# One level of Strassen in the last two large products of an fp32 encoder layer

## The reference, cut to what matters

```
h = rms_norm(x, norm_g)
u = h @ attn_w_in                        # (256 x 4096) @ (4096 x 10240): q, k, v, z
o = windowed attention of q, k, v        # 32 heads of 128, 8 groups of keys, a sink per head
x1 = x + (o * silu(z)) @ attn_w_out      # (256 x 4096) @ (4096 x 4096)   the OUT product
gate = sigmoid(rms_norm(x1, ple_g) @ ple_w_gate)   # (256 x 4096) @ (4096 x 4096)   the GATE product
out = x1 + (p @ ple_w_proj) * gate       # (256 x 256) @ (256 x 4096)     the small product
```

## Time and profile before

| | us |
|---|---|
| median of 3 runs (lowest, highest) | 1695.78 (1695.72, 1696.10) |
| the profiled execution: its own time | 1696.34 |
| its span, first to last instruction | 1694.5 |
| PE busy | 1676.8 (99% of the span) |
| DVE busy | 945.7 (56%) |
| ACT busy | 800.2 (47%) |
| DMA, mean rate | 189 GB/s |

### The profile page before, as it was taken

How to read it: one execution, slowest core, us unless ns; L and a number is a source line. 1 busy time by engine, 2 the same in 40 slices (tenths; PEclk the granted TensorE clock), 3 DMA queues, 4 the chain that set the end, 5 groups by cost and what they waited for, 6 DMA issues and landing times.

```text
span 1694.5 us, 21692 instructions
## 1 busy us (share of the span) xinstructions
PE 1676.8 (99%) x7648; PEld 1394.9 (82%) x7648; DVE 945.7 (56%) x1008; ACT 800.2 (47%) x1002; POOL 65.4 (4%) x49
## 2 busy tenths in 40 slices
PE   7999999999999999999999999999999999999997
PEld 6888888888888888888888888888888888888886
DVE  7654466565756566565656754444446544444445
ACT  7443445454444545455455544444446444444442
POOL 1000000000000000000000000000000000000005
PEclk9999999999999999999999999999999999999999
DMA  8666665656565565656555566666666666566665
GB/s 298 195 189 194 194 180 168 188 158 186 162 184 173 169 178 162 196 155 189 166 174 173 179 207 203 199 199 201 205 199 200 191 193 193 192 197 190 195 193 179
DMA packets 168584, 319.67 MB, mean 189 GB/s; under 512 B 10592, under 2 KB 14944, under 8 KB 168544
## 3 DMA queue, kind: packets, MB, share of 16 engines
q1 hardware_dynamic: 165376, 314.61, 60.8%
q10 hardware_dynamic: 3168, 4.51, 0.8%
HBM read 314.89 MB, written 4.19 MB: 188 GB/s over the span
## 4 chain that ended last, share of the span: by engine, by line
PE 97%; POOL 1%; DVE 1%; ACT 1%; DMA 0%; issue 0%; POOLq 0%; SPq 0%; ACTq 0%
PE bank L860 31%; PE bank L862 31%; PE bank L861 31%; POOL stage L292 1%; PE bank L931 1%; PE bank L883 1%; PE bank L875 1%; PE bank L921 0%; PE bank L920 0%; PE bank L919 0%; PE bank L939 0%; PE bank L941 0%; PE bank L940 0%; DVE w_lo L555 0%; DMA raw<-in_w_in_dram 0%; ACT w_hi L304 0%
## 5 line engine op out<-in xcount | busy, mean ns | idle before, releaser
L555 DVE TENSOR_TENSOR w_lo<-raw,w_hi 128x1024 fp32r<-128x1024 f32 x584 | 715.3, 1226 | 674.2 <-ACT w_hi L304 673.0
L304 ACT ACTIVATE w_hi<-raw 128x1024 fp32r<-128x1024 f32 x584 | 619.3, 1061 | 753.2 <-PE bank L862 748.5
L860 PE MATMUL bank<-w_lo,aT_hi 128*128 128x512 f32 x2304 | 901.9, 391 | 8.5 <-DVE w_lo L555 8.5
L862 PE MATMUL bank<-w_hi,aT_lo 128*128 128x512 f32 x2304 | 897.9, 390 | 0.0
L861 PE MATMUL bank<-w_hi,aT_hi 128*128 128x512 f32 x2304 | 897.5, 390 | 0.0
L860 PEld LDWEIGHTS bank<-w_lo,aT_hi 128*128 128x128 f32 x2304 | 433.3, 188 | 96.5 <-issue 8.5
L862 PEld LDWEIGHTS bank<-w_hi,aT_lo 128*128 128x128 f32 x2304 | 433.1, 188 | 90.7
L861 PEld LDWEIGHTS bank<-w_hi,aT_hi 128*128 128x128 f32 x2304 | 433.5, 188 | 88.2
L278 POOL TENSOR_TENSOR rstd<-ssq,mhalf 128x8 f32<-128x8 f32 x8 | 13.5, 1682 | 790.5 <-DVE ssq L606 790.5
L668 DVE SCALAR_TENSOR_TENSOR arena<-bank,rstd,arena 128x256 f32<-128x256 f32 x64 | 26.6, 478 | 25.2 <-PE bank L921 15.7
L355 ACT ACTIVATE arena<-arena,nm 128x256 f32<-128x256 f32 x64 | 31.8, 499 | 11.8 <-DVE sd L681 11.8
(11 more groups left out here) (92 smaller groups left out, 551.9 us busy)
## 6 DMA issues: line engine op xcount, KB each, us to landing
raw<-in_w_in_dram SPq DMA_DIRECT2D x320, 512.0 KB, 3.7
raw<-in_w_out_dram SPq DMA_DIRECT2D x128, 512.0 KB, 3.7
raw<-in_w_gate_dram SPq DMA_DIRECT2D x128, 512.0 KB, 3.6
stage<-in_xT_dram SPq DMA_DIRECT2D x8, 512.0 KB, 8.2
arena<-in_x_dram ACTq DMA_DIRECT2D x8, 512.0 KB, 6.5
raw<-in_w_proj_dram SPq DMA_DIRECT2D x8, 512.0 KB, 3.6
out_dram<-stage SPq DMA_DIRECT2D x16, 256.0 KB, 2.0
arena<-in_pT_dram ACTq DMA_DIRECT2D x1, 256.0 KB, 2.7
```

The costliest lines, as they stand in the source:

```text
L304: nc.scalar.activation(w_hi[:, i % RING, :], raw[:, i % RING, :], ACT.Copy).then_inc(hi_done, 1)
L555: nc.vector.tensor_tensor(w_lo[:, i % RING, :], raw[:, i % RING, :], w_hi[:, i % RING, :].bitcast(F32), ALU.subtract).then_inc(lo_done, 1)
L860: nc.tensor.matmul(outs[t][:, :], ahi, wlo, start=first and jj == 0, stop=False)
L862: last = nc.tensor.matmul(outs[t][:, :], alo, whi, start=False, stop=final and jj == 1)
```

## The change

Output columns are now taken 1024 at a time (a pair, four in each stage; `PAIRS`), and weights 256 rows by 1024 columns at a time (a quad; 16 to a pair). A dense quad is two units of 12 matmuls. A Strassen quad takes the 2 x 2 blocks of activations (two blocks of channels by two token tiles) and the 2 x 2 blocks of weights, and makes 7 products of sums of blocks in place of 8, in four units of 1, 2, 2 and 2 products. Quads with odd number from 9 on in the first pair of a stage, and from 3 on in the other three pairs, are Strassen quads: 4 + 3 x 7 = 25 in a stage, 50 in all. So dense and Strassen quads alternate.

Each Strassen quad needs four sums of weight blocks. DVE forms them in `T` during the dense quad ahead of it (`weight_sums_1`, `weight_sums_2`), from the raw weights of the Strassen quad. These have to be there earlier, so `plan()` puts the load of a Strassen quad ahead of the load of the dense quad before it. `raw` still has four buffers, which is two quads. `w_hi` and `w_lo` get two more slots (`slot_hi`, `slot_lo`), in tiles that the attention no longer needs. The sums of activation blocks (`ext_hi`, `ext_lo`) are formed once in each stage, by `combos` and the functions after it.

The finished banks of a pair are combined by 12 additions on DVE (OUT) or 8 (GATE). The layer's x1 has no room in SBUF: it is written to the output tensor (`spill`) and read back (`load_x1r`). The small product moves from the end into the GATE stage, two units for each pair; its results go to `pj`, and each finished pair is multiplied, added and stored during the next pair. POOL has no part in it. The order of the splits of the activations changes, too. Cut to its core (a line "..." marks what is left out):

```diff
+def strassen_from(stage, m):
+    return 9 if m == 0 else 3
...
+def plan():
...
+    for k, q in enumerate(line):
+        if q.strassen:
+            if line[k - 1].strassen:
+                loads.append(q)
+            continue
+        if k + 1 < len(line) and line[k + 1].strassen:
+            loads.append(line[k + 1])
+        loads.append(q)
...
+    for k, q in enumerate(loads):
+        q.raw = 2 * (k % 2)
+        q.raw_free = tuple(raw_free[q.raw + h] for h in range(2))
+        for h in range(2):
+            raw_free[q.raw + h] = q.unit + h + 1
...
+            def load_quad(q):
...
+                for h in range(2):
+                    sp.wait_ge(lo_done, q.raw_free[h])
...
+                    sp.dma_start(dst, src).then_inc(raw_in[q.raw + h], 16)
...
+            for k, q in enumerate(loads):
+                load_quad(q)
+                s, m, n = q.stage, q.pair, k % QUADS
+                if n == 3 and s == OUT and m > 0:
+                    spill(m - 1)
...
+                elif n == 6 and s == OUT:
+                    load_x_pair(m)
...
+                elif n == 8 and s == GATE:
+                    if m > 0:
+                        load_x1r(m)
+                    if m < PAIRS - 1:
...
+                        for b in range(2):
+                            load_wp(m + 1, b, wp_raw[b])
+                elif n == 14 and s == GATE and m == 0:
+                    load_x1r(0)
...
-                for t in range(TOK):
-                    pool.wait_ge(gated_proj, TOK * n + t + 1)
-                    pool.tensor_tensor(gates[:, t, cols], gates[:, t, cols], x1[:, t, cols], ALU.add)\
-                        .then_inc(pool_sum, 1)
...
+            def hi_unit(q, h):
+
+                if h < 2:
+                    act.wait_ge(raw_in[q.raw + h], q.raw_count)
+                    src = raw[:, q.raw + h, 0:N] if q.strassen and h == 0 else raw[:, q.raw + h, :]
+                else:
+                    act.wait_ge(t_done, 3 * q.nth + h)
+                    src = T[:, 2 * (h - 2):2 * (h - 2) + 2, :].rearrange("q k n -> q (k n)")
+                act.wait_ge(pe_half, q.slot_free[h])
...
+            def weight_sums_1(q):
+
+                for h in range(2):
+                    dve.wait_ge(raw_in[q.raw + h], q.raw_count)
+                dve.wait_ge(lo_done, q.sums_free)
...
+                nc.vector.tensor_tensor(T[:, 1:3, :], raw[:, q.raw:q.raw + 2, N:2 * N],
+                                        raw[:, q.raw, :].rearrange("q (b n) -> q b n", b=2), ALU.subtract).then_inc(t_done, 1)
+
+            def weight_sums_2(q):
+
+                b21, b22 = raw[:, q.raw + 1, 0:N], raw[:, q.raw + 1, N:2 * N]
+                dve.wait_ge(t_done, 3 * q.nth + 1)
+                nc.vector.tensor_tensor(T[:, 0, :], b22, T[:, 1, :], ALU.subtract).then_inc(t_done, 1)
+                dve.wait_ge(t_done, 3 * q.nth + 2)
+                nc.vector.tensor_tensor(T[:, 3, :], b21, T[:, 0, :], ALU.subtract).then_inc(t_done, 1)
...
+                        for h in range(q.units):
+                            lo_unit(q, h)
+                            if ahead and h == 0:
+                                weight_sums_1(ahead)
+                            elif ahead:
+                                weight_sums_2(ahead)
...
+                                if (pos, h) == (0, 1):
+                                    evacuate_out(before)
...
+                                if (pos, h) == (0, 1):
+                                    evacuate_gate(m - 1)
+                                elif (pos, h) == (1, 1):
+                                    wp_lo_part(m, 1)
+                                    gate_products(m - 1)
...
+            def strassen_unit(q, h, touched, total):
+
+                i = q.i
+                pe.wait_ge(lo_done, ends(q, h))
...
+                steps = (((P1, a_tile(2 * i, 0)),),
+                         ((0, a_tile(2 * i + 1, 0)), (2, ext_tile(i, 2))),
+                         ((P6, ext_tile(i, 1)), (P5, a_tile(2 * i, 1))),
+                         ((P7, ext_tile(i, 0)), (1, a_tile(2 * i + 1, 1))))[h]
+                for n, (k, a) in enumerate(steps):
+                    last = product(q, k, touched, total, a, whi[:, n * N:(n + 1) * N], wlo[:, n * N:(n + 1) * N])
+                last.then_inc(pe_half, 1)
```

More of the change, by code:

```diff
@@ L65, with units, parts @@
 G_OUT = G_Z(N_KV - 1) + 1
-G_GATE = G_OUT + D_MODEL // N
-G_PROJ = G_GATE + D_MODEL // N
 NOUT = D_MODEL // N
-POOL_SUMS = NOUT - 1
-SQUARE_STEPS = (6, 8, 9, 11, 12, 14, 15)
+PAIRS = NOUT // 2
+QUADS = KT // 2
+OUT, GATE = 0, 1
+SLOTS = 6
+N_EXT = QUADS // 2 - 1
+X_CHUNKS, Z_CHUNKS, Y_CHUNKS = (4, 6), (6, 8), (1, 4)
+OUT_OPS, GATE_OPS = 12, 8
+P1, P6, P5, P7 = 4, 5, 6, 7
+SQUARE_STEPS = (6, 8, 9, 11, 12, 14, 15)
+@dataclass
+class Quad:
+    stage: int
+    pair: int
+    pos: int
+    i: int
+    strassen: bool
+    unit: int = 0
+    slots: tuple = ()
+    slot_free: tuple = ()
+    raw: int = 0
+    raw_free: tuple = ()
+    raw_count: int = 0
+    nth: int = 0
+    sums_free: int = 0
+    @property
+    def units(self):
+        return 4 if self.strassen else 2
+    def parts(self, h):
+        if (self.stage, self.pair) == (OUT, 0) and self.pos < 2:
+            return [(2 * h, self.pos), (2 * h + 1, self.pos)]
+        if (self.stage, self.pair, self.pos) == (GATE, PAIRS - 1, QUADS - 1):
+            return [(2 * self.i, h), (2 * self.i + 1, h)]
+        return [(2 * self.i + h, 0), (2 * self.i + h, 1)]
@@ new lines, in strassen_from, with order_of @@
+def strassen_from(stage, m):
+    return 9 if m == 0 else 3
+def order_of(stage, m):
+    if (stage, m) != (GATE, PAIRS - 1):
+        return list(range(QUADS))
+    order = [0, 1]
+    for i in range(3, QUADS, 2):
+        order += [i, i - 1]
+    return order
+def plan():
+    table = [[[Quad(s, m, pos, i, i % 2 == 1 and i >= strassen_from(s, m)) for pos, i in enumerate(order_of(s, m))]
+              for m in range(PAIRS)] for s in (OUT, GATE)]
+    line = [q for s in table for m in s for q in m]
+    loads = []
+    for k, q in enumerate(line):
[6 more added lines that the diff above has]
+        loads.append(q)
+    unit, nth, sums_free = G_OUT * HALVES, 0, 0
+    slot_free = [unit - RING + s + 1 for s in range(RING)] + [0, 0]
+    for k, q in enumerate(line):
+        q.unit = unit
+        if q.strassen:
+            q.slots = (2, 3, 4, 5) if (q.stage, q.pair, q.pos) in ((GATE, 0, 9), (GATE, PAIRS - 1, 2)) else (4, 5, 2, 3)
+            q.nth = nth
+            nth += 1
+            q.sums_free, sums_free = sums_free, unit + 4
+        elif q.pos < 9 and q.pair == 0:
+            q.slots = (2, 3) if q.pos % 2 else (0, 1)
+        else:
+            q.slots = (4, 5) if q.pos == 1 else (0, 1)
+        q.slot_free = tuple(slot_free[s] for s in q.slots)
+        for h, s in enumerate(q.slots):
+            slot_free[s] = unit + h + 1
+        unit += q.units
+    raw_free = [G_OUT * HALVES - RING + s + 1 for s in range(RING)]
+    raw_count = [G_OUT * HALVES // RING] * RING
+    for k, q in enumerate(loads):
[3 more added lines that the diff above has]
+            raw_free[q.raw + h] = q.unit + h + 1
+            raw_count[q.raw + h] += 1
+        q.raw_count = 16 * raw_count[q.raw]
+    return table, loads
@@ L409, in gate_sigmoid, with gate_sigmoids @@
[L409 to L415, removed]
+            def gate_sigmoids(m):
+                for (t, b), op in (((0, 0), 2), ((0, 1), 4), ((1, 0), 7), ((1, 1), 8)):
+                    act.wait_ge(evac, evac_base(GATE, m) + op)
+                    nc.scalar.activation(tile(t, b), tile(t, b), ACT.Sigmoid, scale=r[:, t:t + 1]).then_inc(gate_ready, 1)
@@ L418, in _, with pj_copy @@
+            def pj_copy(m, b):
+                act.wait_ge(proj_ps, 2 * m + b + 1)
+                act.wait_ge(gated, 4 * m)
+                if m == 0 and b == 0:
+                    act.wait_ge(conv_lo, QUADS + 8)
+                for t in range(TOK):
+                    last = nc.scalar.activation(pj(t, b), bank[4 + 2 * b + t][:, :], ACT.Copy)
+                last.then_inc(pj_out, 1)
             act.wait_ge(g1_landed, 16)
@@ L458, in gating, with halve_bias @@
                     z_sigmoid(c)
+            def halve_bias(c):
+                act.wait_ge(scores_sb, c * 2 + 2)
+                nc.scalar.activation(bias, bias, ACT.Copy, scale=0.5).then_inc(bias_ready, 1)
             with act.Fori(0, N_KV - 1) as c:
@@ L519, in _ @@
[L519 to L535, removed]
@@ L550, in _ @@
+            m = PAIRS - 1
+            copy_p1(GATE, m)
+            for k, (t, b) in enumerate(((0, 0), (1, 0), (0, 1), (1, 1))):
+                act.wait_ge(last_sum, k + 1)
+                nc.scalar.activation(tile(t, b), tile(t, b), ACT.Sigmoid, scale=r[:, t:t + 1]).then_inc(gate_ready, 1)
         @block.vector
@@ new lines, in product @@
+            def product(q, k, touched, total, a, whi, wlo):
+                if touched[k] == 0:
```

(7 more changed lines are left out.)

784 lines of the change are left out of this document (554 added, 230 removed).

## The result

The changed kernel takes 1953.03 us (median of 4 runs, 1951.63 to 1955.14) where the kernel before takes 1695.75: ratio 1.1518, 95% interval 1.1498 to 1.1538. It is slower, as forecast, but by 257 us and not by 123; it lies outside the range of 1750 to 1880.

The account below looks back on a forecast made before the run. The prediction took PE, busy 99% of the span, to bound the kernel. The profiled 1696.3 less 34.0 and 3.0 gave 1659.3; + 123.9 - 14 + 19.2 + 28.4 + 2.4 = 1819.2 us, range 1750 to 1880.

Parts of the forecast that it names:

- The signs: Expected in the trace: PE 85 to 90% busy, ACT waiting for loads some 40 times, median landing 5 us or so.
- signs of being wrong: PE at 98 to 99% in pairs 1 to 3, a cycle of 10.2 us, or matmuls inside a unit 0.43 apart.
- The cycle that decides: Supply cycle, counted from a (DVE starting a Strassen quad's first unit): 13.15 us against PE's 10.20; 42 cycles cost +123.9.
- My own rows at the launch: Earlier trace's DMA rates: 287 GB/s from 6 to 12 us, 369 GB/s from 12 to 24 us.
- heavy queue: Rival on weight loads: 1.83 us per load, cycle 13.97 us, total 1862 us; chance 0.08.
- The seven boundaries: Between pairs and into GATE, PE waits for late splits and additions: together +19.2 us (bounds 5 and 40).
- The tail: After PE's last matmul: 5.8 us to the end in place of 8.85, so -3.0 us.
- The transfers ahead of dense loads: Ten 1 MB transfers in SP's queue each delay the dense load by 2.84 us: +28.4 us.
- The run-ahead: In a stage's first pair, supply gets some 7 us ahead of PE, repaid once in each stage: -14 us.
- PE's clock: Rival: gaps drop PE to its lower clock in a third of the 42 cycles, adding 85: about 1904 us; chance 0.08.
- Hidden loads: Rival: supply cycle stays under 10.20 us, PE remains the bound, time 1659 to 1665 us; chance 0.08.

Follow-up runs that it names:

- e1: Changed kernel with each dense quad's load issued ahead of the load of the Strassen quad behind it: 1735.25 us, ratio to before 1.0227.
- e3: Changed kernel with an eighth product of three matmuls in each Strassen quad, giving PE back the 150 saved matmuls: 1949.5 us.
- e4: Changed kernel with the ten 1 MB transfers issued one quad later, behind the dense load: 1935.95 us.
- e5: On top of e1, DVE splits both units of the dense quad before forming the first weight sum: 1691.19 us, ratio to before 0.9968.
- e6: On top of e5, the 1 MB transfers are issued behind a Strassen load, ahead of a dense one: 1686.60 us, ratio to before 0.9945.
- e2: Changed kernel with SP waiting for both buffers of a quad before issuing its first load, so both Strassen halves are issued together: 1924.8 us.
- e7: e6 with the eighth product of e3 (three matmuls more in each of 50 Strassen quads): 1712.67 us.

## Why the prediction was right in kind and wrong in size

**Right.** The mechanism was the one foretold: `raw` two quads deep, the dense load held in SP's queue behind a Strassen load that waits for DVE, and a supply cycle that is longer than PE's 10.20 us. e1 shows it by undoing the order alone. PE's busy share (89%), the matmul count, and the chain through loads and splits are as foretold. The signs were too small: ACT waits for loads 101 times and not some 40, and the median landing is 6.0 to 6.2 us and not 5. One of the signs of being wrong came up too, matmuls 0.43 us apart inside a unit; e3 shows that they don't set the time, so the sign was badly chosen.

**The step that failed** is in "The cycle that decides": "landed 4.45 + 1.42 = 5.87" for the second Strassen half, and with it 7.29 for the dense half behind the two. I took loads in flight to land one behind the other at the full rate of the earlier trace rows. Measured, the second half lands at a + 8.2 (median), 3.6 us behind the first, as long as a whole load takes alone; the loads behind it mostly follow at 1.25, and where it lands early (a + 5.9 to 6.7, in eight cycles) they still come no sooner than a + 8.4. So the dense half lands at a + 9.6 and not at 7.29, and the median cycle is 15.65 us, 2.5 longer than 13.15. My own rows at the launch had the warning: 287 GB/s in the stretch in which loads first came together, 369 only later. I gave "heavy queue" 0.08, and even that case, 13.97, was too light.

**The sum, term by term.** The terms are made from the starts of the 50 first units of Strassen quads. The 42 cycles inside pairs are 673.1 us together, 244.7 over 42 x 10.20. The forecast had 140.7 for the same (123.9 + 28.4 for transfers + 2.4 - 14). The seven boundaries are 248.8 us together against 203.7 by PE's work as the forecast counts it, so +45 where it had +19; the loads of D0 of the next pair come late in the same way (D0's two units wait 1.68 and 2.81 us at 1179.5 and 1183.5 in the boundary looked at). The tail is 8.3 us from the last matmul to the end, not 5.8: the new tail saves 0.5 and not 3.0. From the start of the last bank's addition to the end are 5.8 us, as counted, but that addition starts at 1944.71, 2.5 us behind the last matmul (1942.23), as DVE has a bank's addition, a product and an addition of the tiles before ahead of it. 1694.5 - 34.0 - 0.5 + 244.7 + 45.1 = 1949.8, and the span is 1950.5.

**Terms mis-sized the other way.** The transfers ahead of dense loads cost 17 us (e4), not 28.4. The run-ahead of 14 us isn't to be seen: the three cycles of the first OUT pair are 16.17, 15.66 and 15.38 us like all others. The forecast had the first Strassen quad ready some 7 us before PE wants it. DVE starts on that quad's first unit in OUT, and PE takes it up, at

```profile
1006.20 0.69 DVE L1057 TENSOR_TENSOR qT_lo<-raw,qT_hi 128x512 fp32r<-128x512 f32 x1
...
1008.48 0.39 PE L1492 MATMUL bank<-qT_lo,aT_hi 128*128 128x512 f32 x1
```

so the lead is 2.3 us from the start of the split (0.3 in GATE), no more than in later cycles, and there was nothing to give back.

**The rivals.** PE's clock, at 0.08, happened in part: in the cycle shown PE is at the lower level after its pause of 4.65 us, and over the run the granted clock is 0.949. e3 shows that it isn't what the cycles wait for. The page "TensorE: Matmul & The Clock Gate" of the Trainium skill (HAM oscillation) tells of a kernel that falls to half clock behind the wait for DMA in every step. The trace agrees in kind, in 33 of the 42 cycles, but here it cost nothing that e3 could show, since PE had time to spare. Hidden loads (0.08) were not the case as the kernel stood; e5 and e6 reach that state by order alone and come out at 1691 and 1687, where the forecast put that rival at 1659 to 1665; in e6 the 42 cycles are 429.9 us together, 1.5 over PE's work, and the rest is at the boundaries (227.8 us together, 24 over PE's work) and in the tail (8.0 us and not 5.8).

**What stays open.** Why the second load of a burst is so late. e2 shows that issuing the loads together removes it, and e6 that it is mostly smaller when nothing follows closely. It isn't that a load waits for the end of the one ahead, as the 787 KB above show; in the cycle looked at the loads move at a lower rate together than in e2, and end in a trickle. The engines' mean share of 21% and 3% while the last loads of a burst are still out suggests that a few of the 16 engines finish late. Which, and why, no view of the trace tells, as it has no number for the engine of a packet.

## What to carry to other kernels

In a queue that is issued in order, a load's place matters as much as its size: put the load whose buffer is free ahead of the one that must wait, and count the whole cycle from "buffer free" through queue, landing, copy and split back to "buffer free" before counting what an engine saves. Saved matmuls are worth nothing (e3) or nearly their price (e7), depending on whether that cycle is shorter than PE's. Look for the instructions that stand between a landing and the release of its buffer and do not need it: moving one of 1.14 us was worth 44 us here (e5).

## What the runs showed of the hardware that was not expected

- A 512 KB load issued 1.1 us behind another on an idle queue, with two or more 0.4 us behind it, took 6.4 us to land (median of 42, 4.1 to 7.2; 6.7 in the cycle shown); issued 0.4 us behind the first, it took 4.8 (e2). Four loads issued within 1.3 us landed 1.27 us apart, which is 413 GB/s (524,288 bytes each).
- Issuing a load later can bring all the others earlier: e2 is 28 us faster than the changed kernel.
- After a pause of 4.65 us PE ran 5.3 us at matmuls 0.43 us apart. In e1, where PE's longest wait for a split is 4.1 us and most are far shorter (30 waits, 32.0 us), the granted clock is 0.995.
